# The feed-forward gate row multiplied into the down weights by GpSimd, the second tile's last sums by column halves, and the gate row made behind x's turns

## The reference

```
mod = (silu(c) @ ada_w[layer] + ada_b[layer]).reshape(bsz, 3, 3, D_MODEL)    # per sub-layer: shift, scale, gate
def modulate(t, sub):
    return rms_norm(t, norm_g[layer, sub]) * (1.0 + mod[:, sub, 1]) + mod[:, sub, 0]
def swiglu(h, w_gate, w_up, w_down):
    return (silu(h @ w_gate) * (h @ w_up)) @ w_down

x = x + 0.5 * (1.0 + mod[:, 0, 2]) * swiglu(modulate(x, 0), w_gate, w_up, w_down)    # 1024 -> 2816 -> 1024
x = x + (1.0 + mod[:, 1, 2]) * mixer(modulate(x, 1))
x = x + 0.5 * (1.0 + mod[:, 2, 2]) * swiglu(modulate(x, 2), ...)
...
return rms_norm(x, final_norm_g)
```

## Time and profile before

| | us |
|---|---|
| median of 3 runs | 2357.31 (2352.36 to 2361.34) |
| the profiled execution, its span | 2353.5 |
| TensorE busy | 2226.4 |
| VectorE busy | 1707.6 |
| ACT busy | 1177.1 |
| GpSimd busy | 234.2 |

### The profile page before, as it was taken

How to read it: one execution, slowest core, us unless ns; L and a number is a source line. 1 busy time by engine, 2 the same in 40 slices (tenths; PEclk the granted TensorE clock), 3 DMA queues, 4 the chain that set the end, 5 groups by cost and what they waited for, 6 DMA issues and landing times.

```text
span 2353.5 us, 33775 instructions
## 1 busy us (share of the span) xinstructions
PE 2226.4 (95%) x13726; PEld 1972.1 (84%) x13726; DVE 1707.6 (73%) x2136; ACT 1177.1 (50%) x1390; POOL 234.2 (10%) x183
## 2 busy tenths in 40 slices
PE   7899999998899999997999989899999999989998
PEld 7778888888678888887998987799989988868997
DVE  5667679994667679997776786787677776586555
ACT  3554356883644356874434764433343344534333
POOL 5200312212000302310000010000000020000000
PEclk9899999998999999998999999999999999999999
DMA  9129779994029779995884332488668743206651
GB/s 250 59 95 332 254 270 326 359 359 165 3 101 342 257 271 331 363 355 187 298 277 173 145 130 86 161 290 291 229 236 280 266 151 136 109 1 209 195 180 70
DMA packets 241451, 505.56 MB, mean 215 GB/s; under 512 B 10383, under 2 KB 104529, under 8 KB 241296
## 3 DMA queue, kind: packets, MB, share of 16 engines
q1 hardware_dynamic: 216144, 417.84, 50.7%
q10 hardware_dynamic: 21600, 77.09, 9.2%
q0 software_dynamic: 3552, 8.47, 1.5%
HBM read 502.31 MB, written 1.05 MB: 214 GB/s over the span
## 4 chain that ended last, share of the span: by engine, by line
PE 61%; DVE 9%; ACT 2%; issue 1%; DMA 0%; DVEq 0%; ACTq 0%
PE PS L1091 22%; PE PS L1107 10%; PE PS L926 7%; PE PS L1191 6%; PE PS L884 5%; PE PS L1290 2%; DVE WGL L2349 2%; PE PS L1310 2%; PE PS L1200 1%; PE PS L1354 1%; DVE AR L2352 1%; PE PS L1386 1%; PE PS L1570 1%; DVE XN L2349 1%; DVE AR L2349 1%
## 5 line engine op out<-in xcount | busy, mean ns | idle before, releaser
L2349 DVE TENSOR_TENSOR WGL<-ring,WGH 128x2048 fp32r<-128x2048 f32 (+1 forms) x291 | 599.8, 2069 | 226.2 <-ACT WGH L1778 116.9
L1091 PE MATMUL PS<-XTB,WGH 128*128 128x256 f32 x2816 | 516.3, 285 | 5.3 <-DVE XTB L2349 4.9
L1091 PEld LDWEIGHTS PS<-XTB,WGH 128*128 128x128 f32 x2816 | 447.5, 193 | 15.9 <-issue 8.1
L1091 PE MATMUL PS<-XTB,WGL 128*128 128x256 f32 x1408 | 400.0, 284 | 0.0
L1091 PEld LDWEIGHTS PS<-XTB,WGL 128*128 128x128 f32 x1408 | 271.6, 193 | 0.0
L2349 DVE TENSOR_TENSOR WDL<-ring,WDH 128x1024 fp32r<-128x1024 f32 (+1 forms) x136 | 216.9, 1595 | 32.3 <-ACT WDH L1945 22.9
L1945 ACT ACTIVATE WGH<-ring 128x2048 fp32r<-128x2048 f32 x96 | 183.4, 1914 | 102.6 <-PE PS L1191 39.6
L1778 ACT ACTIVATE WGH<-ring 128x1024 fp32r<-128x1024 f32 (+2 forms) x107 | 145.1, 1360 | 178.9 <-PE PS L926 61.1
L926 PE MATMUL PS<-XTB,WGH 128*128 128x256 f32 x1088 | 206.4, 291 | 12.6 <-DVE WGL L2349 9.8
L1988 ACT ACTIVATE XN<-PS 128x256 f32<-128x256 f32 x88 | 33.8, 384 | 352.4 <-PE PS L1091 326.8
L926 PEld LDWEIGHTS PS<-XTB,WGH 128*128 128x128 f32 x1088 | 173.2, 195 | 23.8 <-DVE WGL L2349 11.6
(11 more groups left out here) (522 smaller groups left out, 4450.6 us busy)
## 6 DMA issues: line engine op xcount, KB each, us to landing
FA<-in_ada_w ACTq DMA_DIRECT2D x144, 512.0 KB, 6.3
ring<-in_moe_w_up SPq DMA_DIRECT2D x64, 1024.0 KB, 7.0
ring<-in_moe_w_gate SPq DMA_DIRECT2D x64, 1024.0 KB, 7.9
ring<-in_moe_w_down SPq DMA_DIRECT2D x64, 1024.0 KB, 7.6
ring<-in_ffn_w_gate SPq DMA_DIRECT2D x44, 1024.0 KB, 5.8
ring<-in_ffn_w_up SPq DMA_DIRECT2D x44, 1024.0 KB, 10.3
ring<-in_ffn_w_down SPq DMA_DIRECT2D x44, 1024.0 KB, 7.4
ring<-in_hyb_w_in SPq DMA_DIRECT2D x10, 1152.0 KB, 6.6
```

Of the source, the lines that this page charges most:

```text
L1091: ins = mm(PS[:, 4 + b, m * T:(m + 1) * T], w_[:, b, w], x_[:, k, :], start=k == 0 and q == 0, stop=k == KD - 1 and q == 2)
L2349: return V.tensor_tensor(out_, x_, y_, op)
```

## The change

- **The multiply.** In each feed-forward stage GpSimd waits for the gate row (`row`) and then goes through all 22 tiles: when an item's down weights have landed it multiplies each tile's 128x1024 raw weights in the ring by ROWB[:, 0], in place (new line 820, `dn_gated`). ACT's high part of down now waits for `dn_gated` instead of `w_land`. PSY is then already gated.
- **The residual** (`residual`, was `residual_gate`). In a feed-forward stage there is no multiply: VectorE adds PSY to X. Row tile 1 is added in two halves of 512 columns, here and in hyb and mlstm (where the multiply stays and is halved too).
- **Halves on TensorE.** In `last_downs`, and in the last piece of hyb and mlstm, the products of row tile 1 come by column halves, and a new semaphore `y_half` is raised behind the first.
- **The squares.** ACT squares and sums row tile 1 by halves: the first sum goes through a step of its own to the bias of the root.
- **The gate row earlier.** The diagonals are made right behind `begin`, ahead of `split_x`; the gate row's matmuls stand behind x's turns and ahead of gate_up 0, into banks 0 and 1; ACT copies it ahead of the first high part of down.
- **The last modulation turn** of a feed-forward stage is summed into bank 0 after row tile 0 has been added, and written by VectorE in the `begin` of the next stage.

```
+                if r.kind == "ffn":
+                    pool.wait_ge(S("row"), r.v2 + 1)
+                    if FINAL and r is plan[-1]:
+                        ld(ROWB[:, 1, :], a["final_norm_g_2"].partition_broadcast(P), "late_load")
+                    for j in range(CH * r.items):
+                        s = (r.n + j // CH) % SLOTS
+                        _, dn = raw_slot(r, j)
+                        pool.wait_ge(S(f"w_land{s}"), LANDS[r.n + j // CH])
+                        nc.gpsimd.tensor_tensor(dn, dn, ROWB[:, 0, :], ALU.mult).then_inc(S("dn_gated"), 1)
...
                     rows(j + 1, 0, (0, 1, 2)).then_inc(S("y0"), 1)
-                    rows(j, 1, (1, 2)).then_inc(S("w_used"), 1)
-                    rows(j + 1, 1, (0, 1, 2)).then_inc(S("w_used"), 1)
+                    rows(j, 1, (1, 2), (0,))
+                    rows(j + 1, 1, (0, 1, 2), (0,)).then_inc(S("y_half"), 1)
+                    rows(j, 1, (1, 2), (1,)).then_inc(S("w_used"), 1)
+                    rows(j + 1, 1, (0, 1, 2), (1,)).then_inc(S("w_used"), 1)
...
                 if r.name in LAST_TURN:
-                    mod_sums(LAST_TURN[r.name], PS[:, 6, 0:AW // P])
+                    if r.kind == "ffn":
+                        pe.wait_ge(S("xres"), TT + 3 * r.v2 + 1)
+                    mod_sums(LAST_TURN[r.name], PS[:, 0 if r.kind == "ffn" else 6, 0:AW // P])
...
             def ffn(r):
                 trn(r.u, XN)
-                hidden_layer(r, lambda: gate_row(r))
+                gate_row(r, 0)
+                hidden_layer(r)
...
+                    if t and halves:
+                        summed(t, slice(0, 512), SSQ[:, t:t + 1])
+                        f(SQ0, SSQ[:, t:t + 1], ACT.Identity, bias=EPSC[:, 1:2]).then_inc(S("ssq"), 1)
+                        count["ssq"] += 1
+                        summed(t, slice(512, 1024), SQ1)
+                        f(SD[:, t:t + 1], SQ1, ACT.Sqrt, bias=SQ0).then_inc(S("sd"), 1)
...
-                    act.wait_ge(S(f"w_land{s}"), LANDS[r.n + j // CH])
+                    act.wait_ge(S("dn_gated"), r.cb + j + 1)
...
                 split_high(r, 1, True)
+                gate_row_out(r, 0)
...
                 split_high(r, 0, False)
...
-                for t in range(TT):
+                for t, cols in ((0, slice(0, D)), (1, slice(0, 512)), (1, slice(512, D))):
                     if t == 0:
                         dve.wait_ge(S("y0"), work.index(r) + 1)
+                    elif cols.start == 0:
+                        dve.wait_ge(S("y_half"), r.v2 + 1)
                     else:
                         dve.wait_ge(S("w_used"), r.we)
-                    c(tt(XN[:, t, :], PSY[:, t, :], ROWB[:, 0, :]))
-                    tt(X[:, t, :], X[:, t, :], XN[:, t, :], ALU.add).then_inc(S("xres"), 1)
+                    y = PSY[:, t, cols]
+                    if r.kind != "ffn":
+                        c(tt(XN[:, t, cols], y, ROWB[:, 0, cols]))
+                        y = XN[:, t, cols]
+                    tt(X[:, t, cols], X[:, t, cols], y, ALU.add).then_inc(S("xres"), 1)
...
             def ffn(r):
                 begin(r)
+                diagonals(r)
                 split_x(r)
                 first_low(r, 1)
-                diagonals(r)
```

More of the change, by code:

```diff
@@ L878, in out_piece @@
                 by_k = [(k, t) for k in range(2) for t in range(TT)]
-                for k, t in sorted(by_k, key=lambda x: x[1]) if last else by_k:
-                    if last and k == 0 and t == 1:
+                halves = last and r.kind in ("hyb", "mlstm")
+                parts = [(k, t, (0, 1)) for k, t in (sorted(by_k, key=lambda x: x[1]) if last else by_k)]
+                if halves:
+                    parts = parts[:2] + [(k, 1, (h,)) for h in range(2) for k in range(2)]
+                for n, (k, t, hs) in enumerate(parts):
+                    if last and n == 2:
                         ins.then_inc(S("y0"), 1)
+                    if halves and n == 4:
+                        ins.then_inc(S("y_half"), 1)
                     for q, (x_, w_) in enumerate(((XTH, hi), (XTH, lo), (XTL, hi))):
-                        for h in range(2):
+                        for h in hs:
                             ins = mm(PSY[:, t, 512 * h:512 * h + 512], x_[:, k0 + k, t * P:(t + 1) * P],
@@ L1073, in odd, with hidden_layer @@
                 out_rows(r)
-            def hidden_layer(r, beside):
+            def hidden_layer(r):
                 turn = MOD_TURNS.get(r.name)
@@ L1098, in ready, with rows @@
                     pe.wait_ge(S("hidden"), r.cb + j + 1)
-                def rows(j, t, terms):
+                def rows(j, t, terms, halves=(0, 1)):
                     last = not exists(r, j, 1)
@@ L1105, in rows @@
                         h_, w_ = ((HTH, WDH), (HTH, WDL), (HTL, WDH))[q]
-                        for h in range(2):
+                        for h in halves:
                             ins = mm(PSY[:, t, 512 * h:512 * h + 512], h_[:, b, t * P:(t + 1) * P],
@@ L1133, in hidden_layer @@
                     if turn is not None and j % 5 == 4 and j < 15:
-                        if j == 4:
-                            pe.wait_ge(S("row"), r.v2 + 1)
                         sums_by_token(turn + j // 5)
@@ L1723, in norm_roots, with summed, root_of_squares @@
                         f(X[:, 0, :], X[:, 0, :], ACT.Identity, scale=RSTD[:, 0:1], bias=NMR0).then_inc(S("xn0"), 1)
-            def root_of_squares():
+            def summed(t, cols, dst):
+                count["xres"] += 1
+                act.wait_ge(S("xres"), count["xres"])
+                f(XN[:, t, cols], X[:, t, cols], ACT.Square, scale=D ** -0.5, accum_out=dst).then_inc(S("ssq"), 1)
+                count["ssq"] += 1
+                act.wait_ge(S("ssq"), count["ssq"])
+            def root_of_squares(halves):
                 f(ST[0:1, 94:95], EPSC[0:1, 1:2], ACT.Sqrt)
                 for t in range(TT):
-                    count["xres"] += 1
-                    act.wait_ge(S("xres"), count["xres"])
-                    f(XN[:, t, :], X[:, t, :], ACT.Square, scale=D ** -0.5, accum_out=SSQ[:, t:t + 1])\
-                        .then_inc(S("ssq"), 1)
-                    act.wait_ge(S("ssq"), count["xres"])
-                    f(SD[:, t:t + 1], SSQ[:, t:t + 1], ACT.Sqrt, bias=EPSC[:, 1:2]).then_inc(S("sd"), 1)
+                    if t and halves:
+                        summed(t, slice(0, 512), SSQ[:, t:t + 1])
+                        f(SQ0, SSQ[:, t:t + 1], ACT.Identity, bias=EPSC[:, 1:2]).then_inc(S("ssq"), 1)
+                        count["ssq"] += 1
+                        summed(t, slice(512, 1024), SQ1)
+                        f(SD[:, t:t + 1], SQ1, ACT.Sqrt, bias=SQ0).then_inc(S("sd"), 1)
+                    else:
+                        summed(t, slice(0, D), SSQ[:, t:t + 1])
+                        f(SD[:, t:t + 1], SSQ[:, t:t + 1], ACT.Sqrt, bias=EPSC[:, 1:2]).then_inc(S("sd"), 1)
             def softplus_exp(e, a_):
@@ L1757, in squares @@
             def squares(r):
-                root_of_squares()
+                root_of_squares(r.before.kind != "moe")
             def high(r, p):
@@ L1789, in prepare, with gate_row_out @@
                     high(r, 1)
-            def gate_row_out(r):
+            def gate_row_out(r, bank=6):
                 act.wait_ge(S("row_ps"), r.v2 + 1)
-                f(ROWB[:, 0, :], PS[:, 6:8, :].rearrange("p j n -> p (j n)"), ACT.Copy).then_inc(S("row"), 1)
+                f(ROWB[:, 0, :], PS[:, bank:bank + 2, :].rearrange("p j n -> p (j n)"), ACT.Copy).then_inc(S("row"), 1)
             def attention(r, units):
@@ L2453, in residual_norm, with last_turn_out @@
                 mark().then_inc(S("x_ready"), 1)
+            def last_turn_out(r):
+                if r.kind == "ffn" and r.name in LAST_TURN:
+                    mod_out(LAST_TURN[r.name], PS[:, 0, 0:AW // P])
             def begin(r):
@@ L2459, in begin @@
                     ts(XN[:, t, :], X[:, t, :], RSTD[:, t:t + 1]).then_inc(S(f"xn{t}"), 1)
+                last_turn_out(r.before)
                 if not early(r):
@@ L3233, in mlstm @@
                 modulation(r)
-                residual_gate(r)
+                residual(r)
             def final():
```

25 lines of the change are left out of this document (8 added, 17 removed).

## The result

The changed kernel took 2388.86 us (median; 2386.4 to 2393.95) against 2357.87 for the kernel before on the same chip: a ratio of 1.0138, 95% interval 1.0123 to 1.0154. It is slower by 31 us; the forecast was 2399, 10 us too high.

A forecast was written before the change was run, and what follows sets the result against it. TensorE was taken to bound the feed-forward stages. Turns +34.8, starts +14.0, feed-forward ends -6.0, hyb and mlstm -0.8 gave +42.0 on the 2353.5 us span, 2395.5; plus 3.8 to the median, 2399 us, range 2358 to 2425.

The forecast's parts named there:

- What bounds the kernel, and that the multiplies hold VectorE: Feed-forward stages: TensorE bounds; GpSimd multiplies hold VectorE's instructions with two SBUF inputs, not those reading PSUM.
- The cast: VectorE's 0.29 us SBUF cast in each tile: taken as held by a multiply; without that the sum some 10 us lower.
- The turns: Five-tile turns: VectorE plus GpSimd need 46.3 us against TensorE's 43.4; 11.6 us per modulated stage, 34.8 for three.
- the ACT load of the next modulation piece: Modulated turns: a VectorE instruction held for 2.39 us also holds this load, which waits for the product; no separate size.
- The starts: Start of each feed-forward stage: multiplies delay down 0, 2.6 us in ffn10, 3.8 in each other, 14.0 in all.
- The ends: Last product to x scaled: 1.5 us gained in each of four feed-forward stages, 6.0; hyb and mlstm 0.4 each, 0.8.
- (d): Stage ends: ACT's longer queue takes back all of the 6.8 gained, 2406; chance 0.62 together with the forecast.
- What would show it: Profile after: multiplies median some 4 us, down products waiting, some 5 us idle at down 0, ends about 3.7 us.
- a WGL mean of 2.3 us: VectorE's low part of gate and up: this mean in the profile after would make the forecast wrong outright.
- (b): No contention in the feed-forward stages, so gate row and ends only gain: -11 us, 2346; chance 0.12.
- (a): Only the starts cost; in the turns PSUM instructions and VectorE's waits take up the multiplies: +7, 2364; chance 0.15.
- (c): Modulated turns: late low parts delay landings, pairs always fall on product tiles; 19 us a stage, +64, 2421; chance 0.11.

The follow-up runs named there:

- Paced: The changed kernel with each GpSimd multiply of tile j (from 2 on) also waiting for hidden tile j - 2, one a tile: 2360.29 us, ratio 1.0011.
- behind_late: The changed kernel with one multiply per tile let go by WGL, plus ACT's second ada_w load issued behind WGH of tile j + 2: 2345.55 us, 0.9946.
- behind_wgl: The changed kernel with each tile's multiply let go by VectorE's low part WGL of the same tile: 2401.65 us, ratio 1.0184.
- start_only: The changed kernel with only the multiplies of tiles 2 and 3 waiting for the hidden vector of two tiles before: 2383.32 us, ratio 1.0106.
- ghost: The kernel before plus the 88 GpSimd multiplies on an unused tile, at the same landings; only the residual waits for them: 2415.29 us, ratio 1.0247.
- noprod: The changed kernel with seven of eight modulation products of each turn left out in ffn00, ffn01 and ffn10: 2360.84 us, ratio 1.0020.
- one_input: The kernel before plus 88 unused GpSimd instructions with one SBUF input (tensor_scalar) in place of multiplies by ROWB: 2357.05 us, ratio 0.9999.

## Why the prediction was right, and where it wasn't

- **What bounds the kernel, and that the multiplies hold VectorE.** Right. The operations that I took as held are held, and those that read PSUM aren't. The cast, which I took as held without a row, is: 0.29 to 2.06 us. By the Trainium skill (VectorE: DVE Perf Modes, section "Mode 2×_2P — use both read ports for one tensor") an SBUF to SBUF copy can take both of VectorE's read ports, the two-port mode of which the prediction spoke; the 2.06 agrees.
- **The turns: 34.8 forecast, 32.5 measured, and the step behind it was wrong.** I made the sum of two engines that take turns, 46.3 us against 43.4, and let the difference be the cost. Paced has the same multiplies at +9.7 and behind_late at +2.1, so there is room for them. Two things stood against the sum. A multiply may lie in time that VectorE waits anyway or spends on PSUM. And the bound was not VectorE's total, but closed loops: in behind_wgl the one through ACT's queue that I had named in half a sentence ("and the ACT load of the next modulation piece, which waits for the product") and then not followed; in the changed kernel this one for 10 us, and for the rest, as far as argued above, the one through the load into FA. That the size came out within 3 us is luck: behind_wgl, with starts of the reduction 46.4 us apart (1593.76, 1640.17), just meets the 46.3, yet 3.9 of that is waiting (3 x 1.30), which leaves 42.5 of work, under 43.4.
- **A part of the 32.5 is TensorE's clock.** See the last section; at most some 8 us, by the surplus length of its matmuls at four places in the turns: 1.7 in ffn00, 2.8 in ffn01, 1.7 and 1.5 in ffn10, at granted clocks of 0.75, 0.62, 0.72 and 0.76 over 6 to 7 us. No step of mine had it.
- **The starts: 14.0 forecast, 9.0 measured.** The mechanism was right: four multiplies in a row, 12.28 us, with WDL, cast and HTL held between them, and start_only takes it away. Over-sized by half: TensorE idled 3.3 and 3.4 us ahead of down 0 in ffn01 and ffn10 and 1.7 in ffn00 and ffn11, not some 5. I had set 2.6 for ffn10 (measured 1.7) and 3.8 for the others (2.1, 2.9, 2.2).
- **The ends: -6.0 forecast, -7.1 measured**, hyb and mlstm -0.8 as forecast. Rival (d) fell. Here is ACT at the end of ffn01, with the last product ending at 1735.43:

```profile
1736.88 0.62 ACT L1740 ACTIVATE XN<-X 128x512 f32<-128x512 f32 x1
1737.40 0.19 ACT L1740 ACTIVATION_READ_ACCUMULATOR XN<-X 128x1 f32 x1
1737.62 0.29 ACT L1753 ACTIVATE ST<-ST 128x1 f32<-128x1 f32 x1
```

  ACT was the last one, as I counted, and 0.2 us earlier than I counted.
- **What would show it.** Down products waiting for HTL, not in ffn11's turns, multiplies with a minimum of 2.38 and a median of 2.95 us (I said some 4), ends of 3.5: as written. But I had also written that a WGL mean of 2.3 us would make the forecast wrong outright, and the mean is 2.287. That sign was badly chosen. It took the one VectorE instruction of the earlier trace rows for all of them, and did not ask at which place of VectorE's list a landing falls.
- **Rivals.** (b), no contention, is refuted by ghost. (a), only the starts cost, is nearly what noprod does (starts +8.7, turns +4.3), and not what the change does. (c), late landings that feed on themselves: the pairs came where something was held each time, but the turns stayed at little over half its 57 us.

## What to carry to other kernels

When an engine is given work that holds another, ask first which closed loop the held one is in, and what that loop has to spare against the beat of the bounding engine; its idle time over a stage says nothing on that (here 44 us in a stage, but 0.3 us in a tile's loop). If a queue in order, as ACT's here, waits to issue a load into a buffer, it makes everything behind the load a part of the loop: put the load behind what others wait for, if it can still land in time. And place the added work by a wait that lets it fall in the held engine's own idle time, rather than by the landing of a load.

## What the runs showed of the hardware that I had not expected

**The clock after a wait.** The down products of ffn01 begin after 3.3 us of waiting, in noprod as in the changed kernel, and then run at about half speed. Noprod in two stretches (busy time of each engine, then the granted clock, DMA share, GB/s):

```profile
1527.00:1533.00 6.00, 2.76 (x23) 2.55 (x22) 5.93 (x5) 3.13 (x4) 5.61 (x2) 0.89 0.49 153
1533.00:1539.00 6.00, 5.96 (x17) 4.83 (x18) 4.95 (x7) 1.96 (x2) 0.00 (x0) 0.54 0.35 108
```

The granted clock is 0.54 in the second stretch, most of it at the lower level, 1.2 GHz, after one in which TensorE was busy 2.76 of 6 us; in behind_late, which has no such wait, it is 1.00 on both sides of its first down product. Two down products take 1.05 us instead of 0.63, and the stretch costs 2.7 us: all that noprod's turns lose in ffn01. A wait of 3.3 us so cost 6 in all. In ffn10 a wait of 3.6 us is followed by 3.1 us at the lower level, and the turns lose 1.5; in ffn00 and ffn11, where the wait is 1.6, the clock stays at 1.00 and they lose nothing.

**Whole instructions.** By the Trainium skill (SBUF — State Buffer, "SBUF: two separate sides") GpSimd and VectorE hold their shared ports for a whole instruction; that agrees with all rows above, but the price of a held instruction was mostly set elsewhere, by what stood behind it.

**One-input GpSimd work is held and holds too.** In one_input VectorE's HTL, WDL and cast have longer means (600, 1299, 395 ns in ffn00) beside a GpSimd instruction with one SBUF input. I had thought either possible.

**What stays open.** Why ghost costs 22 us more in the turns than the changed kernel, with the same pairs at the same landings, wasn't separated. One difference in its trace: its first four multiplies of ffn01 fall on the first HTL (2.64 us), on a WGL (4.48) and on the first product of the turn (2.88), those of the changed kernel on WDL, cast and HTL. Another: in ffn01 and ffn10 one pair of nine falls on cast and HTL alone, in the changed kernel four; the others hold a product or WDL, which stand in the loops. And its turns spend 24 us at the lower clock, against 16. None of them was tried by itself. Nor did I try whether the move of the load alone changes the kernel before.
